# Experts of a two-layer hybrid decoder: gathered rows by block and quarter turned on VectorE, gate-up weights in four parts

## The chip, the cores and the metric

One core of one Trainium2 chip. The metric is the device time of the program in microseconds (us); lower is better. The inputs are float32, and all matmuls run in float32.

## The reference

Two decoder layers over 1024 tokens of width 1024. Layer 0 mixes sliding-window attention with a Mamba-2 scan, layer 1 is a Conformer convolution module. After each mixer comes the part that the change touches, a mixture of 32 SwiGLU experts with hierarchical routing:

```
g_sel = argmax(xt @ w_group + b_group)                    # one of 4 groups per token
eid   = g_sel * 8 + top_k(e_logits of that group, 2)      # two of its 8 experts
gu    = xb @ w_gate_up[e]                                 # 1024 -> 2 x 512
out   = (silu(gu[:, :512]) * gu[:, 512:]) @ w_down[e]     # 512 -> 1024
y[token] += gate * out                                    # 2048 (token, expert) pairs
x = x + y
```

An expert's gate-up weights are 4 MB and its down weights 2 MB; 32 experts in each of two layers make some 400 MB, all of which are read once.

## The kernel before, in words

`moe(k, layer)` runs once per layer, with every engine's program written out in full. Two stages matter here.

**Routing.** TensorE computes the logits (L1416), VectorE the choice of experts, the rank of each pair within its expert and, from a table of tokens by rank that TensorE makes (L1434), two index tables: `hidx`, the row of the normalised tokens `hbuf` (in HBM) that each partition gathers for an expert, and `yidx`, the quarter row of `ybuf` that each partition writes. `row_index` (L1590) makes `hidx` for the fixed experts first and for the others later. `sort_weights` (L1642) then gives `order`, the experts in the order in which they are processed. The first three places (`FIXED`) belong to experts 0, 1 and 2 whatever the router says; the other 29 are sorted by their number of tokens, so that the capacity of each place is known when the program is built: 2, 3 or 4 blocks of 32 tokens (`TB`), 84 blocks in all. Tokens beyond a capacity would go through `over`, a loop that does not run with these inputs. `count_overflow`, `place_overflow` and `index_overflow` (L1656 to L1687) make its tables and set `over_ready`.

**Experts.** For each expert q, 128 whole rows are gathered by GpSimd's queue (`gather`, L1349, three buffers `xg`), turned on TensorE by eight 128x128 transposes (`turn_tokens`, L1450) and brought from PSUM to `xT` by VectorE with the gain `g_exp` (`xT_evacuate`, L1629). Per block n of 32 tokens follow `gate_up(n)` on TensorE (64 matmuls in eight steps of the inner dimension by four groups of columns, with rhs the weights: 32 x 256; L1468), silu on ScalarE (L1294), the product and a 32x32-block transpose on VectorE (`hidden`, L1636 and L1640), `down(n)` on TensorE (L1483), a copy on ScalarE (L1288) and a scatter of quarter rows by GpSimd's queue (L1356). TensorE's order is: all gate-up blocks of expert q, the turning of q + 1, all down blocks of q. A float32 matmul shows twice in the trace, so that one block of gate-up counts 64 and one of down 32.

The weights come through SyncE's queue, in program order: four places for gate-up (`wgu`: `early_gu`, two in `wgu`, and the residual's own room `x_res`, which is parked in HBM meanwhile) and three for down (`wd`). `load_gate_up` (L1182) is one DMA of 4 MB with 32 KB per partition; it waits until the last block of the expert that had the place, four earlier, is through gate-up (`gu_done`). `load_down` (L1185) waits for `d_done` of the expert three earlier. The first load behind the fixed ones needs `order_ready`. The place `wd[2]` holds the router's tables first, so that expert 2's down weights wait for `over_ready`.

```
for q in range(FIXED, BOUND):
    e = sp.value_load(order[0:1, q:q + 1], min_val=0, max_val=NE - 1)
    if q > FIXED:
        sp.wait_ge(gu_done, last_of[gu_user[q]] + 1)
    load_gate_up(sp, e, gu_of[q])
```

## Time and profile before

| what | value |
|---|---|
| median of 3 runs | 2039.64 us (2038.15 to 2040.13) |
| the profiled execution: its span | 2039.7 us |
| TensorE busy | 1861.9 us (91%) |
| VectorE / ScalarE / GpSimd busy | 883.6 / 427.2 / 405.6 us |
| HBM read and written | 504.29 and 43.03 MB |
| experts of layer 0, first gate-up to last down | 546.1 to 1038.1 us |
| experts of layer 1, first gate-up to last down | 1504.0 to 1996.9 us |

The profiled execution has no time of its own beside its span; the span lies 0.1 us from the median, within the spread of the runs, so that the span is taken as the time. The busy share of TensorE is of its matmul queue. In the forty slices of the page each slice is 51 us; the two stretches of experts are the ones in which DMA stands at 9. An idle time that ends with "issue" is one whose end the profile puts down to no other engine.

### The profile page before, as it was taken

What the parts mean: (1) busy time and instruction counts of PE and PEld (TensorE: products, weight loads), DVE (VectorE), ACT (ScalarE), POOL (GpSimd) and SP (SyncE); (2) the same over time, 40 slices, a digit from 0 to 9 for tenths busy, and PEclk for the clock granted to TensorE, in tenths of its full rate; (3) what the DMA queues carried; (4) which work ended last, traced back from release to release, by engine and by line L of the source; (5) the groups of instructions that cost most, each with busy time, mean ns of one, the idle gap of its engine ahead of it and who ended that gap; (6) DMA issues with size and microseconds to landing.
All of it is one profiled execution on the core that took longest, in us unless ns stands there. A gap on an engine that the chain in (4) does not pass through costs nothing. (4 is left out here: it accounts for less than half of the span.)

```text
span 2039.7 us, 46987 instructions
## 1 busy us (share of the span) xinstructions
PE 1861.9 (91%) x20566; PEld 1141.8 (56%) x20566; DVE 883.6 (43%) x1980; ACT 427.2 (21%) x965; POOL 405.6 (20%) x524
## 2 busy tenths in 40 slices
PE   7999999999699999988959999799869999999891
PEld 5677766665466666555645444345546666655551
DVE  3666666564811211111135999893271121121114
ACT  2433332345011111110123122233401111111010
POOL 2211111012122222222122011120112222212120
PEclk9999999999699999999979999899979999999996
DMA  9300000044699999999987446413589999999997
GB/s 324 81 11 1 11 10 10 0 186 168 267 426 426 427 424 427 425 425 427 421 310 195 92 103 134 108 32 134 206 332 422 425 425 426 424 426 428 425 405 276
DMA packets 94256, 541.95 MB, mean 266 GB/s; under 512 B 23366, under 2 KB 46970, under 8 KB 76392
## 3 DMA queue, kind: packets, MB, share of 16 engines
q1 hardware_dynamic: 68376, 479.13, 57.3%
q0 software_dynamic: 23040, 51.43, 9.1%
q10 hardware_dynamic: 2640, 8.44, 1.0%
q8 instruction: 160, 2.62, 0.5%
q14 instruction: 40, 0.33, 0.1%
HBM read 504.29 MB, written 43.03 MB: 268 GB/s over the span
## 5 line engine op out<-in xcount | busy, mean ns | idle before, releaser
L1636 DVE TENSOR_TENSOR acts<-acts,ps 128x128 f32<-128x128 f32 x168 | 66.1, 393 | 781.3 <-ACT acts L1294 780.9
L1356 POOL DMA_INDIRECT y_rows<-rows_in_out,yidx x168 | 166.7, 992 | 747.3 <-ACT rows_in_out L1288 720.5
L1468 PE MATMUL ps<-wgu,xT 128*32 128x256 f32 x5376 | 297.7, 381 | 9.8 <-issue 9.7
L1468 PEld LDWEIGHTS ps<-wgu,xT 128*32 128x32 f32 x5376 | 181.7, 110 | 120.9 <-issue 13.1
L1483 PE MATMUL ps<-wd,acts 128*32 128x256 f32 x3520 | 198.6, 380 | 0.0
L1468 PE MATMUL ps<-x_res,xT 128*32 128x256 f32 x2816 | 159.2, 387 | 16.6 <-issue 16.6
L1294 ACT ACTIVATE acts<-ps 128x128 f32<-128x128 f32 x168 | 46.6, 277 | 608.0 <-PE ps L1468 608.0
L1468 PE MATMUL ps<-early_gu,xT 128*32 128x256 f32 x2560 | 146.7, 389 | 7.9 <-DVE xT L1629 4.1
L1483 PEld LDWEIGHTS ps<-wd,acts 128*32 128x32 f32 x3520 | 110.9, 110 | 74.8 <-issue 6.7
L1468 PEld LDWEIGHTS ps<-x_res,xT 128*32 128x32 f32 x2816 | 96.3, 112 | 77.6 <-issue 22.5
L2232 DVE SCALAR_TENSOR_TENSOR conv<-dd,par,conv 128x256 f32<-128x256 f32 (+1 forms) x255 | 131.4, 589 | 0.2
L1288 ACT ACTIVATE rows_in_out<-ps 128x256 f32<-128x256 f32 x168 | 64.4, 384 | 304.5 <-PE ps L1483 304.5
L1468 PEld LDWEIGHTS ps<-early_gu,xT 128*32 128x32 f32 x2560 | 85.0, 113 | 66.9 <-issue 10.1
L865 PEld LDWEIGHTS ps<-m_hT,early_gu 128*128 128x128 f32 x1024 | 116.1, 192 | 4.7 <-issue 3.3
L865 PE MATMUL ps<-m_hT,early_gu 128*128 128x128 f32 x1024 | 116.9, 275 | 0.7 <-DMA early_gu<-in_w_in 0.7
L1859 PE MATMUL ps<-c_hT,early_wd 128*128 128x512 f32 x256 | 114.4, 600 | 3.4 <-ACT sig L2020 3.2
L1895 PE MATMUL ps<-w_pw,c_hT 128*128 128x512 f32 x256 | 114.4, 602 | 1.5 <-ACT c_hT L2037 1.5
L1867 PE MATMUL ps<-c_hT,early_wd 128*128 128x512 f32 x256 | 112.5, 592 | 0.0
L1483 PE MATMUL ps<-early_wd,acts 128*32 128x256 f32 x1856 | 104.7, 380 | 0.0
L919 PE MATMUL ps<-w_out_sb,m_yT 128*128 128x512 f32 x192 | 86.3, 602 | 0.0
L1859 PEld LDWEIGHTS ps<-c_hT,early_wd 128*128 128x128 f32 x256 | 49.0, 192 | 65.4 <-issue 65.0
L1867 PEld LDWEIGHTS ps<-c_hT,early_wd 128*128 128x128 f32 x256 | 48.7, 190 | 61.2 <-issue 61.2
(354 smaller groups left out, 2225.1 us busy)
## 6 DMA issues: line engine op xcount, KB each, us to landing
wgu<-in_moe_w_gate_up SPq DMA_DIRECT2D x32, 4096.0 KB, 30.8
wd<-in_moe_w_down SPq DMA_DIRECT2D x42, 2048.0 KB, 30.4
early_gu<-in_moe_w_gate_up SPq DMA_DIRECT2D x18, 4096.0 KB, 30.7
x_res<-in_moe_w_gate_up SPq DMA_DIRECT2D x14, 4096.0 KB, 28.8
early_wd<-in_moe_w_down SPq DMA_DIRECT2D x22, 2048.0 KB, 26.4
early_wd<-in_conv_w_pw SPq DMA_DIRECT2D x22, 512.0 KB, 5.5
conv<-prod POOLq DMA_DIRECT2D x20, 512.0 KB, 4.5
x_res<-x_park SPq DMA_DIRECT2D x2, 4096.0 KB, 45.9
```

The source lines that it names most:

```text
L865: mm = pe.matmul(ps[:, bank, (t % 4) * P:(t % 4 + 1) * P], w_x[:, j, t * P:(t + 1) * P], hT[:, j, :], start=(j == 0), stop=(j == KD - 1))
L919: mm = pe.matmul(ps[:, bank, :], attn_T[p][:, j, :] if j < 4 else yT[:, j, :], w_out[:, j, 512 * half:512 * half + 512], start=(j == 0), s ...
L1288: act.activation(y[:, n % YB, :], ps[:, Y + n % 2, 0:D // 4], ACT.Copy).then_inc(y_ready, 1)
L1294: act.activation(sg[:, n % 2, :], ps[:, GU + n % 2, 0:P], ACT.Silu).then_inc(silu_ready, 1)
L1356: pool.indirect_dma_start(out=y_quarters, out_offset=bass.IndirectOffsetOnAxis(ap=yidx[:, tl, q:q + 1], axis=0), in_=y[:, n % YB, :], in_o ...
L1468: mm = pe.matmul(ps[TB * g:TB * g + TB, GU + n % 2, 0:2 * P].rearrange("p (a f) -> p a f", a=2), xT[:, q % 2, j, TB * tl:TB * tl + TB], wg ...
L1483: mm = pe.matmul(ps[TB * g:TB * g + TB, Y + n % 2, 0:D // 4], hhT[:, n % 4, TB * j:TB * j + TB], wd[q % 3][:, j, D // 4 * g:D // 4 * g + D ...
L1636: tt(hh[:, n % 2, :].rearrange("q (k f) -> q k f", k=KF), by_k(sg[:, n % 2, :]), by_k(ps[:, GU + n % 2, P:2 * P]), ALU.mult).then_inc(hh_r ...
L1859: mm = pe.matmul(ps[:, GATE, :], wg[:, p, j, :], hT[:, j, HALF * h:HALF * h + HALF], start=(j == 0), stop=(j == KD - 1))
L1867: mm = pe.matmul(ps[:, LIN + n % 2, :], wa[:, p, j, :], hT[:, j, HALF * h:HALF * h + HALF], start=(j == 0), stop=(j == KD - 1))
L1895: mm = pe.matmul(ps[:, BACK + half, :], yT[:, j, :], w_pw2[:, j, 512 * half:512 * half + 512], start=(j == 0), stop=(j == CT - 1))
L2232: ins = dve.scalar_tensor_tensor(out=out[s], in0=dd[:, s, q + k0:q + k1], scalar=par[:, c, 2 * q - 1 + s:2 * q + s], in1=out[s] if r else ...
```

## The change

- **Blocks instead of experts.** `hbuf` is stored in another order within a row (`stored_row`), so that a quarter of a row holds what 32 partitions need. `gather(n)` now fetches for one block of 32 tokens their four quarter rows, one per group of 32 partitions (128 partitions x 256 values, eight buffers), with `hidx` in the form that `yidx` had. 85 gathers take the place of 32.
- **Turning on VectorE.** `prepare(n)` is a 32x32-block transpose of 128x256 and a product with the gain. It takes the place of TensorE's eight transposes and of `xT_evacuate`. The first five blocks are prepared before the loop (three ahead of `sort_weights`, two behind it), then block n + 5 behind `hidden(n)`.
- **Gate-up in four parts.** Each load is four DMAs of 1 MB (8 KB per partition), each with its semaphore, and each part is loaded as soon as TensorE has used that part of the place's former expert (`gu_part_done`). `gate_up(q)` runs part by part over all blocks of the expert, so that all its blocks are finished in the last part. Four PSUM banks hold them, and four the down blocks.
- **A fourth fixed expert** with room for four blocks; its weights are loaded ahead of `order_ready`. There are 85 blocks in place of 84.
- `index_overflow` runs before the first `hidden`, not behind it.

```diff
-FIXED, FULL, LARGE = 3, 2, 13
-XB, YB = 3, 6
-TURNS, LAST_FULL = 12, 17
+FIXED_CAP = (3 * TB, 3 * TB, 3 * TB, 4 * TB)
+FIXED, FULL, LARGE = len(FIXED_CAP), 2, 12
+PARTS = 4
+XB, YB = 8, 6
+PREPARED = 5
+TURNS, LAST_FULL = 12, 16
...
+        def load_gate_up(sp, e, q):
+            user = gu_user[q]
+            for r in range(PARTS):
+                if user is not None:
+                    if r < PARTS - 1:
+                        sp.wait_ge(gu_part_done, (PARTS - 1) * user + r + 1)
+                    else:
+                        sp.wait_ge(gu_done, last_of[user] + 1)
+                load_gate_up_part(sp, e, gu_of[q], r)
...
             sp.wait_ge(x_parked, 16 * (SQUARED_EARLY + 1))
+            load_gate_up(sp, 3, 3)
             sp.wait_ge(order_ready, 1)
-            down = 2
+            down = FIXED - 1
             for q in range(FIXED, BOUND):
                 e = sp.value_load(order[0:1, q:q + 1], min_val=0, max_val=NE - 1)
-                if q > FIXED:
-                    sp.wait_ge(gu_done, last_of[gu_user[q]] + 1)
-                load_gate_up(sp, e, gu_of[q])
+                load_gate_up(sp, e, q)
                 if q == FIXED:
                     sp.wait_ge(over_ready, 1)
-                else:
-                    sp.wait_ge(d_done, last_of[q - 4] + 1)
+                    load_down(sp, 2, 2)
+                sp.wait_ge(d_done, last_of[q - 4] + 1)
                 load_down(sp, down, (q - 1) % 3)
...
+            def gate_up(q):
+                blocks = range(first_of[q], last_of[q] + 1)
+                if q == 0:
+                    pe.wait_ge(first_gu_loaded, 16)
+                for r in range(PARTS):
+                    if q:
+                        pe.wait_ge(gu_loaded[gu_of[q]][r], 16 * (gu_turn[q] - (gu_of[q] == 0)))
+                    for n in blocks:
+                        if r == 0:
+                            pe.wait_ge(xT_ready, n + 1)
+                            if n >= 4:
+                                pe.wait_ge(hh_ready, n - 3)
+                        for j in range(KD // PARTS * r, KD // PARTS * (r + 1)):
...
+                        if r == PARTS - 1:
+                            mm.then_inc(gu_done, 1)
+                    if r < PARTS - 1:
+                        mm.then_inc(gu_part_done, 1)
...
-            turn_expert(0)
             for q in range(NE):
-                for n in range(first_of[q], last_of[q] + 1):
-                    gate_up(n)
-                if q + 1 < NE:
-                    turn_expert(q + 1)
+                gate_up(q)
                 for n in range(first_of[q], last_of[q] + 1):
                     down(n)
...
+            def prepare(n):
+                dve.wait_ge(gathered[n % XB], 16 * (n // XB + 1))
+                if n >= XB:
+                    dve.wait_ge(gu_done, n - XB + 1)
+                dve.transpose(xT[:, n % XB, :, :].rearrange("p k t -> p (k t)"), xg[:, n % XB, :]).then_inc(xg_turned, 1)
+                dve.wait_ge(xg_turned, n + 1)
+                tt(xT[:, n % XB, :, :], xT[:, n % XB, :, :], g_exp[:, :].unsqueeze(2).to_broadcast([P, KD, TB]), ALU.mult).then_inc(xT_ready, 1)
...
+            for n in range(CAP[0] // TB):
+                prepare(n)
             sort_weights()
-            dve.wait_ge(turned, 1)
-            xT_evacuate(0, CAP[0], xT_ready)
+            for n in range(CAP[0] // TB, PREPARED):
+                prepare(n)
             count_overflow()
             place_overflow()
+            index_overflow()
             for n in range(NB):
                 q, tl = blocks_of[n]
                 hidden(n)
-                if n == last_of[q] and q + 1 < NE:
-                    dve.wait_ge(turned, q + 2)
-                    xT_evacuate((q + 1) % 2, CAP[q + 1], xT_ready)
-                if n == 0:
-                    index_overflow()
+                if n + PREPARED < NB:
+                    prepare(n + PREPARED)
```

How instructions stand on TensorE at the start of the experts of layer 0, in the kernel before (L1437 to L1442 are the index matmuls, L1450 the turning, L1468 gate-up, L1483 down):

```order
L1437 MATMUL ps<-early_gu,wd 128x3
L1440 MATMUL ps<-wd 128x32
L1442 MATMUL ps<-wd,rows_in_out 128x32 x4
L1450 MATMUL ps<-ident,rows_in_out 128x2x4x16 x8
L1468 MATMUL ps<-early_gu,xT 32x256 x96
L1450 MATMUL ps<-ident,rows_in_out 128x2x4x16 x8
L1483 MATMUL ps<-early_wd,acts 32x256 x48
L1468 MATMUL ps<-wgu,xT 32x256 x96
```

and in the change (L1463 and L1467 index, L1484 gate-up, L1502 down):

```order
L1463 MATMUL ps<-early_gu,rows_in_out 128x4 x4
L1467 MATMUL ps<-wd,rows_in_out 128x32 x4
L1484 MATMUL ps<-early_gu,xT 32x256 x96
L1502 MATMUL ps<-early_wd,acts 32x256 x48
L1484 MATMUL ps<-wgu,xT 32x256 x96
L1502 MATMUL ps<-wd,acts 32x256 x48
```

The turning is gone between gate-up and down, and the first index takes four matmuls where it took one. VectorE at the same place, from the second index to the overflow tables, in the kernel before (L1643 and L1644 sort, L1629 the move of expert 0's tokens to `xT`):

```order
L1625 TENSOR_SCALAR yidx<-acts,quarter 128x128
L1643 TENSOR_REDUCE wd<-wd 128x32
L1644 CAST order<-wd 128x32
L1629 TENSOR_TENSOR xT<-ps,g_exp 128x4x96 x2
L1658 MEMSET wd 128x3
```

and in the change (L1643 and L1645 are one `prepare`, L1658 and L1659 the sort):

```order
L1637 TENSOR_SCALAR yidx<-acts,quarter 128x128
L1643 STREAM_TRANSPOSE xT<-rows_in_out 128x256
L1645 TENSOR_TENSOR xT<-xT,g_exp 128x256
L1643 STREAM_TRANSPOSE xT<-rows_in_out 128x256
L1645 TENSOR_TENSOR xT<-xT,g_exp 128x256
L1643 STREAM_TRANSPOSE xT<-rows_in_out 128x256
L1645 TENSOR_TENSOR xT<-xT,g_exp 128x256
L1658 TENSOR_REDUCE wd<-wd 128x32
L1659 CAST order<-wd 128x32
```

The sort stands behind three prepared blocks. SyncE's queue around the first sorted expert, in the change (in the kernel before, the `x_res` load stood behind the TENSOR_LOAD of `order`):

```order
L1230 DMA token_slot<-pad 128x32
L1213 DMA wd<-in_moe_w_down 128x4096
L1200 DMA wgu<-in_moe_w_gate_up 128x2048 x8
L1200 DMA x_res<-in_moe_w_gate_up 128x2048 x4
L1241 TENSOR_LOAD order
```

The load of expert 3's gate-up weights has moved ahead of the wait for the order.

## Rows read from the trace of the kernel before

**Rows 1.** The page of the profile: busy tenths of DMA in forty slices of 51 us
```profile
DMA  9300000044699999999987446413589999999997
```

**Rows 2.** Table of stretches: us, busy (x instructions) per engine, PEclk, DMA share, GB/s
```profile
600.00:700.00 100.00, 100.00 (x1768) 60.62 (x1764) 19.42 (x52) 11.42 (x35) 21.28 (x22) 1.00 1.01 425
...
900.00:1000.00 100.00, 92.88 (x1608) 57.35 (x1604) 16.57 (x44) 10.56 (x32) 21.04 (x21) 0.98 1.01 425
```

**Rows 3.** DMA queues and issues between 610 and 960 us
```profile
q1 hardware_dynamic: 6282, 136.17, 90.9%
...
wgu<-in_moe_w_gate_up SPq DMA_DIRECT2D x12, 4096.0 KB, 37.1
```

**Rows 4.** Timeline of TensorE, layer 0: start us, us, instruction [idle before]
```profile
546.13 12.06 PE L1468 MATMUL ps<-early_gu,xT 128*32 128x256 f32 x192 [1.96 <-DVE xT L1629]
...
863.55 10.57 PE L1468 MATMUL ps<-wgu,xT 128*32 128x256 f32 x192 [1.27 <-issue]
...
897.40 12.22 PE L1468 MATMUL ps<-x_res,xT 128*32 128x256 f32 x192 [5.42 <-issue]
...
1027.53 7.11 PE L1468 MATMUL ps<-early_gu,xT 128*32 128x256 f32 x128 [1.41 <-issue]
1034.43 3.66 PE L1483 MATMUL ps<-wd,acts 128*32 128x256 f32 x64
```

**Rows 5.** Timeline of SyncE's queue, layer 0
```profile
498.25 1.76 SPq L1182 DMA_DIRECT2D wgu<-in_moe_w_gate_up  x2
546.23 0.36 SPq L1182 DMA_DIRECT2D x_res<-in_moe_w_gate_up  x1
...
823.83 0.33 SPq L1182 DMA_DIRECT2D wgu<-in_moe_w_gate_up  x1
```

**Rows 6.** Table of stretches around the start of layer 0's experts
```profile
528.00:530.00 2.00, 0.41 (x1) 0.00 (x0) 1.79 (x4) 0.51 (x1) 0.00 (x0) 0.50 0.01 4
...
556.00:558.00 2.00, 2.00 (x44) 0.96 (x32) 1.65 (x5) 0.00 (x0) 0.00 (x0) 1.00 0.65 270
```

**Rows 7.** Timeline of all engines, layer 0's index and start
```profile
528.52 0.42 DVE L1572 TENSOR_TENSOR wd<-ps,wd 128x256 f32<-128x256 f32 x1 [0.18 <-PE ps L1428]
...
534.87 0.59 PE L1437 MATMUL ps<-early_gu,wd 128*128 128x3 f32 x2 [0.49 <-DVE wd L1587]
...
540.52 1.89 PE L1442 MATMUL ps<-wd,rows_in_out 128*128 128x32 f32 x8
...
544.97 0.18 DVE L1644 CAST order<-wd 128x32 int32<-128x32 f32 x1
...
552.76 0.40 DVE L1636 TENSOR_TENSOR acts<-acts,ps 128x128 f32<-128x128 f32 x1
553.19 0.31 DVE L1640 STREAM_TRANSPOSE acts<-acts 128x128 f32<-128x128 f32 x1
...
556.84 0.17 DVE L1686 CAST pos<-posf 128x16 int32<-128x16 f32 x1
```

**Rows 8.** Chain that ended last, layer 1: start us, us, what
```profile
1556.44 10.36 PE ps L1468 x192
1566.81 1.02 PE ps L1450 x8
1567.83 5.32 PE ps L1483 x96
1573.14 6.91 PE ps L1468 x128
```

**Rows 9.** DMA queues and issues between 1450 and 1462 us
```profile
q10 hardware_dynamic: 144, 1.05, 21.1%
...
h_rows<-prod ACTq DMA_DIRECT2D x1, 1024.0 KB, 3.9
```

**Rows 10.** Table of stretches, end of layer 1's experts
```profile
1995.00:2000.00 5.00, 3.58 (x68) 1.97 (x60) 0.70 (x2) 1.04 (x3) 1.68 (x2) 1.00 0.18 74
```

**Rows 11.** DMA issues between 412 and 430 us
```profile
early_gu<-in_moe_w_gate_up SPq DMA_DIRECT2D x1, 4096.0 KB, 13.2
```

More of the change, by code:

```diff
@@ L72, in capacities @@
     n = NE - FIXED
-    by_place = [3 * TB] * FIXED + [0] * n
+    by_place = list(FIXED_CAP) + [0] * n
     for nth in range(n):
@@ L1225, in _ @@
                 down = sp.value_load(order[0:1, q:q + 1], min_val=0, max_val=NE - 1)
-                sp.wait_ge(gu_done, last_of[gu_user[q]] + 1)
-                load_gate_up(sp, down, gu_of[q])
+                load_gate_up(sp, down, q)
             sp.wait_ge(d_done, last_of[NE - 4] + 1)
@@ L1436, in _ @@
             pe.wait_ge(tab_ready, 1)
-            pe.matmul(ps[:, SPREAD, 0:FIXED], tabT[:], fold[:, 0:FIXED], start=True, stop=True).then_inc(spread, 1)
-            pe.wait_ge(tab_ready, 3)
+            for b in range(P // TB):
+                mm = pe.matmul(ps[:, SPREAD, b * FIXED:(b + 1) * FIXED], tabT_rows[:, b, :], fold[:, 0:FIXED], start=True, stop=True)
+            mm.then_inc(spread, 1)
             pe.wait_ge(fold_ready, 1)
-            pe.matmul(ps[:, TOTALS, 0:NE], tabT[:], fold_sorted[:], start=True, stop=True).then_inc(spread, 1)
             for b in range(P // TB):
@@ L1443, in _ @@
             mm.then_inc(spread, 1)
-            def turn_tokens(buf, done, by_rank=True):
-                for j in range(KD):
-                    columns = ps[:, TRN + j // 4, (j % 4) * P:(j % 4 + 1) * P]
-                    if by_rank:
-                        columns = columns.rearrange("p (b h t) -> p h b t", h=2, t=TB // 2)
-                    mm = pe.transpose(columns, xg[:, buf, j * P:(j + 1) * P], ident[:])
-                mm.then_inc(done, 1)
-            def turn_expert(q):
-                pe.wait_ge(gathered[q % XB], 16 * (q // XB + 1))
-                if q:
-                    pe.wait_ge(xT_ready, 2 * q)
-                turn_tokens(q % XB, turned)
@@ L1496, in over @@
             def over(j):
-                pe.wait_ge(o_gathered, j * 16 + 16)
-                turn_tokens(0, o_turned, by_rank=False)
+                pe.wait_ge(o_ordered, j + 1)
+                for i in range(KD):
+                    mm = pe.transpose(ps[:, TRN + i // 4, (i % 4) * P:(i % 4 + 1) * P], over_by_k[:, i * P:(i + 1) * P], ident[:])
+                mm.then_inc(o_turned, 1)
                 pe.wait_ge(o_xT, j * 2 + 2)
@@ L1657, in count_overflow @@
                 cap = cap_e[:, FIXED:NE]
-                dve.memset(cap_e[:, 0:FIXED], float(CAP[0])).then_inc(dve_link, 1)
-                link.n += 1
+                for e in range(FIXED):
+                    dve.memset(cap_e[:, e:e + 1], float(CAP[e])).then_inc(dve_link, 1)
+                link.n += FIXED
                 link(ts(cap, nth[:], float(FULL + LARGE), float(TB), ALU.is_lt, ALU.mult))
@@ L1709, in over @@
                 tt(over_ih[:], over_slot[:], over_h[:], ALU.add).then_inc(o_index, 1)
+                dve.wait_ge(o_gathered, j * 16 + 16)
+                dve.tensor_copy(over_by_k.rearrange("q (k g l) -> q g k l", k=KD, g=4), stored_row(over_x)).then_inc(o_ordered, 1)
                 dve.wait_ge(o_turned, j + 1)
-                xT_evacuate(0, P, o_xT)
+                for half in range(2):
+                    tt(over_xT[:, 4 * half:4 * half + 4, :], ps[:, TRN + half, :].rearrange("p (k t) -> p k t", k=4),
+                       g_exp[:, 4 * half:4 * half + 4].unsqueeze(2).to_broadcast([P, 4, P]), ALU.mult).then_inc(o_xT, 1)
                 dve.wait_ge(o_silu, j + 1)
```

182 lines of the change are left out of this document (87 added, 95 removed).

## Prediction

> **What bounds the kernel now.** I read the page's forty slices first, since an average over the span hides the stages. DMA stands at 9 in nine slices in a row in the first stretch of experts and in the same way in the second [rows 1]. The table of stretches then puts numbers to it: in layer 0 from 600 to 700 us TensorE is busy all the time, DMA's share is 1.01 at 425 GB/s, and from 900 to 1000 TensorE is busy 92.88 of 100 us while DMA stands at the same 1.01 and 425 GB/s [rows 2]. So two resources run close together, and it is DMA that does not give way. The view of the queues says what it carries: 90.9% weights, a gate-up load of 4096 KB taking 37.1 us from issue to landing [rows 3], far more than its own 4.19 MB / 425 GB/s = 9.9 us, so about two and a half experts' weights stand in the queue all the time.
>
> The timeline of TensorE shows the consequence. Expert 0 starts at 546.13; later TensorE waits ("issue") for 5.42 us before 897.40 and for 1.41 us before its last gate-up at 1027.53 [rows 4]. The load issued at 823.83 [rows 5] is the one used at 863.55, after a wait of 1.27 [rows 4]: asked for 40 us ahead, and still late. So these are waits for weights. An expert of three blocks costs TensorE 10.36 + 1.02 + 5.32 = 16.7 us, the 1.02 being the turning [rows 8]. The change takes the turning away, 31 x 1.02 = 32 us per layer of TensorE's time. If TensorE were the bound, that would be the gain, less one more block (half of 6.91 for gate-up and a third of 5.32 for down, 5.2 us) [rows 8]. But it isn't: the stage ends when the last weights have landed, and a faster TensorE only waits longer. So I count the time of the weight queue, per layer, from the router to the last gate-up load.
>
> **The change, part by part**, in us per layer, plus is slower.
>
> *The queue starts later behind the router: +4.3.* Before, the first sorted load is issued at 546.23 [rows 5], right behind the cast of `order` at 544.97 [rows 7]. Now the first index needs one copy of 512 columns and four matmuls: four such took 1.89 against 0.59 for one, while the copy was made anyway, behind the index [rows 7]. With the waits around them, everything behind moves by 1.5. Three `prepare` stand ahead of the sort. None is in the trace; the transpose of 128x128 took 0.31 and a product of 256 columns 0.42 [rows 7], so with twice the columns I take 0.45 + 0.42 + 0.08 for the semaphore = 0.95, and 2.85 for three (bounds: 0.31 + 0.42 each, and twice the small transpose plus 0.62, so 2.2 to 3.9). The cast comes at 549.3, the issue at 550.5: +4.3. The load also needs TensorE's first quarter of expert 0: start at about 546.3, three blocks' quarter 10.36 / 4 = 2.6, and 1.5 that the half clock costs (12.06 against 10.57 [rows 4]; the clock stood at 0.50 before, [rows 6]), so 550.4, which is as late.
>
> *One gate-up load leaves that queue: -9.9.* Expert 3's weights are asked for at about 515, when DMA still works on the 8.4 MB of gate-up (and 2.1 of down) issued at 498 [rows 5]. DMA then stood at 0.01 from 528 to 530 [rows 6] and the weights idle until 546.23. Its 9.9 us fit into that hole.
>
> *Smaller packets: +7.0.* 28 loads go in rows of 8 KB in place of 32 KB. The nearest row with 8 KB rows is the store of 1.05 MB that took 21.1% of 16 engines in 12 us [rows 9]: 40.5 engine-us, 0.316 per row, 1.26 per 32 KB. The weights in large rows took 90.9% x 16 x 350 = 5090 for 136.17 MB, 1.225 per 32 KB [rows 3]. The difference, 0.04, times 128 rows / 16 engines is 0.3 per load. One is a store and the other a load, so the bounds are 0 and 0.4; I take 0.25, near the row, and 28 of them.
>
> *Gathers: 0.* 85 in place of 32, but of the same filled rows in all, and empty ones are skipped. On GpSimd, whose 22 instructions took 21.28 us [rows 2], 85 + 85 at that price are 165 us of 492. On VectorE 85 x 0.95 = 81 replace some 62 moves of 0.4 to 0.5 in a stage where it is busy 17 of 100 us [rows 2]. Both hide below TensorE; what if not, is a rival.
>
> *Pauses of the queue: +1.7.* Before, DMA fell to 0.65 only at 556 to 558 [rows 6], 0.7 us. Now five `prepare` and all overflow tables stand ahead of the first `hidden`: `over_ready`, at 557.0 before [rows 7], comes at 549.3 + 12.0 - 1.0 (the old move) - 0.75 (the first `hidden`) + 1.9 = 561.5. By then the queue has just finished expert 4's quarters, so that costs nothing. TensorE, through gate-up at 558.2, gets its first down operand at 562.4, 4.2 late, and pays 1.5 for the clock again; expert 3's down weights wait for the end of expert 0's down at 569.2, when the queue has been empty for 2.0. With 0.4 for quarters paced by TensorE: 2.4 - 0.7.
>
> *The engines end more evenly: -2.5.* At layer 1's end DMA falls from full to 0.18 over 1995 to 2000 [rows 10] while the last loads land: the sixteen engines don't have equal work, and a load lands with the slowest. Gathers of whole rows give a row to one engine; quarters give it to four partitions 32 apart. The bounds are 0 and 5, half of what the tail shows; I take the middle.
>
> *The tail: -0.3.* After the last gate-up landed TensorE took 1034.43 + 3.66 - 1027.53 = 10.6 [rows 4]. Now only a quarter of gate-up is left, but the down weights land 2.1 MB / 425 GB/s = 4.9 behind, then 3.66 follow: 8.6, and 1.7 because TensorE has waited and runs at half clock, as after 5.42 of idling (12.22 against 10.57 [rows 4]).
>
> Sum: 4.3 - 9.9 + 7.0 + 1.7 - 2.5 - 0.3 = +0.3 per layer, +0.6 for two. The stores of the rows in another order, an activation cut in two four times in layer 1, and the longer-lived semaphores are hidden by ScalarE's and the conformer's slack and cost nothing (at most 0.3 each if that were gone). On the profiled execution's 2039.7 this gives 2040.3, and since that span stands 0.1 above the median of the runs I give 2040.5, no change. A measurement of this kernel can tell about 0.2%, 4.1 us, from none.
>
> **Two rules of the Trainium skill.** A load of 4096 KB alone on the chip landed 13.2 us after issue [rows 11], and one of 1024 KB in 3.9 [rows 9]; but in the stage loads stand behind one another at 425 GB/s [rows 2], so the fixed part of each hides in the queue, and the sum has 0 for it. "DMA: Bandwidth & Descriptors", section "Bandwidth", asks for DMAs of 1 MiB or more, and its "Anatomy of one DMA" gives 2.0 us plus bytes / 436 GB/s for each. By an estimate from that page four loads of 1 MB, one after another, would take 6 us more than one of 4, 168 us per layer. The parts are at the page's limit, and that is a rival below.
>
> The rows tell that the engines end unevenly, not which has which partition. The same page, "The descriptor swizzle", gives engine = 8 x (partition / 64) + (partition / 4) mod 8. By an estimate from that map and these inputs' token counts the busiest engine's excess falls from 16 to 11 us in layer 0 and from 12 to 9 in layer 1; with that in place of 2.5 the result would be 2037.5. No run so far shows the map.
>
> **The rivals.** *The packets cost nothing and the engines end evenly: faster.* For it speaks that the price of 8 KB rows comes from a store. With 0 and -5 the layer gives 0.3 - 7.0 - 2.5 = -9.2, and half-way, which I hold for more likely, -5: 2030. Chance 0.28.
>
> *The queue pays more: slower.* One mechanism: the weights' queue runs dry early in the stage, while TensorE paces it. Each quarter waits for TensorE, and TensorE for `hidden(0)`, itself behind 18 us of VectorE's own list. If `prepare` is at its bound (3.9 for three, 6.5 for five) and rows of 8 KB at 0.4, then +1.1 + 1.4 + 4.2, and no evening gives 2.5 back: some +9 per layer, up to 2058; I give it 2050. It decides once the first quarter of expert 4 is issued after about 554. Chance 0.22.
>
> *VectorE becomes what each expert waits for: slower.* All blocks of an expert now end within the last part, 0.86 apart, and the first down needs silu, product and transpose, of which the last two took 0.40 and 0.31 [rows 7]: with silu and the waits some 1.3 behind, an estimate. For experts of two blocks this leaves 0.5 of waiting where the turning's 1.02 was; I reckon it hidden, since TensorE needs 85 x 5.2 + 32 x 0.14 + 5.7 + 8 = 460 of 492. The slack is 32 us over 32 experts: it decides once each expert loses 1 us more. At 1.5 more it costs 16 per layer, 2072. Against it: VectorE has 1.7 per block to do where TensorE takes 5.2. Chance 0.08.
>
> *Each part pays its fixed time: slower.* If only 0.3 of the 3.9 - 2.5 = 1.4 showed per part, 28 x 3 x 0.3 = 25 per layer, 2090. Against it stands 425 GB/s with queued loads. Chance 0.05.
>
> **How the numbers follow.** No change has 0.37, and its own range is 2036 to 2045. Faster by over 0.2% is the first rival, 0.28; slower the other three, 0.35. The range leaves out the two dear rivals and the far tail of the first: 2027 to 2057.
>
> **What would show it.** Right: DMA's share 1.0 from about 570 to 1020 in layer 0; the fixed load issued at about 515 and the next at 550.5; TensorE waiting some 30 us per layer, mostly before down; the last gate-up part landing within 3 us of 1028; no turning on TensorE and about 460 us busy. Wrong: TensorE busy to the end (then a stall of the blocks, not DMA, is the bound), a q1 share per byte above 1.26 per 32 KB, DMA gaps beyond 570, or a GB/s away from 425.

## The result: 0.57% slower, and the profile after

| | before | changed |
|---|---|---|
| median, us (lowest to highest, 4 runs each) | 2039.61 (2038.15 to 2040.13) | 2050.78 (2046.99 to 2052.37) |
| profiled execution: span, us | 2039.7 | 2048.6 |
| granted TensorE clock, mean | 0.957 | 0.946 |

The ratio is 1.0057, with a 95% interval of 1.0043 to 1.0071: 11.2 us slower, clear of the 0.2% that a measurement can tell. The forecast was no change (2040.5). The slower side came: inside the whole range of 2027 to 2057, outside the 2036 to 2045 that went with no change, and at the time that I had given to the rival "the queue pays more", though not by its mechanism.

The page's slices of DMA, after. The high digits are as in [rows 1]; the second line, GB/s, is where the two kernels differ, mostly 415 to 418 in the two stretches of experts where 421 to 428 stood, and 405 and 397 early in the first:
```profile
DMA  9200000044899999999987456413599999999997
GB/s 324 80 11 1 11 10 10 0 185 177 320 405 397 416 417 417 418 417 416 422 314 208 87 112 134 108 32 134 201 376 402 416 415 416 417 418 418 417 413 291
```
The table of stretches of the changed kernel (us, busy time of PE, PEld, DVE, ACT and POOL, PE's clock, DMA share, GB/s), against [rows 2], and as its last row the whole of layer 0's experts:
```profile
600.00:700.00 100.00, 99.08 (x1829) 58.97 (x1825) 26.69 (x76) 12.61 (x39) 39.56 (x39) 1.00 1.00 406
900.00:1000.00 100.00, 86.39 (x1456) 54.57 (x1448) 21.00 (x60) 9.94 (x30) 28.37 (x28) 0.91 1.01 418
...
545.00:1045.00 500.00, 463.52 (x8160) 282.52 (x8160) 130.62 (x379) 56.26 (x170) 169.16 (x166) 0.96 0.99 405
```
DMA is as full as before (1.01), but it moves 418 GB/s in place of 425: full and slower. TensorE has less to do (86.39 of 100 us where it had 92.88), and it waits for the rest. The busy share alone would have hidden the loss.

DMA queues and issues of the changed kernel between 610 and 960 us, against [rows 3]:
```profile
q1 hardware_dynamic: 15056, 131.97, 90.9%
...
wgu<-in_moe_w_gate_up SPq DMA_DIRECT2D x40, 1024.0 KB, 33.2
y_rows<-rows_in_out,yidx POOLq DMA_INDIRECT x61, 7.4
```
The weights' queue has the same 90.9% of sixteen engines as before for 131.97 MB in place of 136.17. That is 90.9% x 16 x 350 / (131.97 MB / 32 KB) = 1.264 us per 32 KB, against 1.225.

Start and end of layer 0 on TensorE's timeline of the changed kernel, against [rows 4] (the number in brackets is the idle time before):
```profile
545.15 13.50 PE L1484 MATMUL ps<-early_gu,xT 128*32 128x256 f32 x192 [2.80 <-DVE xT L1645]
560.96 7.07 PE L1502 MATMUL ps<-early_wd,acts 128*32 128x256 f32 x96 [2.31 <-DVE acts L1655]
...
910.73 6.42 PE L1502 MATMUL ps<-wd,acts 128*32 128x256 f32 x64 [5.30 <-issue]
...
1034.37 1.93 PE L1484 MATMUL ps<-early_gu,xT 128*32 128x256 f32 x32 [1.15 <-DMA early_gu<-in_moe_w_gate_up]
1039.29 5.30 PE L1502 MATMUL ps<-wd,acts 128*32 128x256 f32 x64 [2.98 <-issue]
```
TensorE starts a microsecond earlier (545.15, before 546.13) and ends later: its last down is through at 1039.29 + 5.30 = 1044.6, before at 1034.43 + 3.66 = 1038.1. The waits now stand mostly before a down, as 5.30 at 910.73, and the half clock that follows makes a two-block down 6.42 or 5.30 long in place of 3.66.

SyncE's queue at the start, against [rows 5]:
```profile
514.24 2.25 SPq L1200 DMA_DIRECT2D x_res<-in_moe_w_gate_up  x4
550.71 8.50 SPq L1200 DMA_DIRECT2D early_gu<-in_moe_w_gate_up  x4
```
The fixed load went out at 514.24 and the first quarter of expert 4 at 550.71, as forecast (515 and 550.5).

### The profile page after: what moved, and what is told of

Read it like the earlier page. It is cut to its first block and busy times, and to the rows that moved or that the text cites. A ratio compares the mean times of both kernels' runs of the same rounds, so it can differ in the third digit from the quotient of the medians.

```text
span 2048.6 us, 47486 instructions
## 1 busy us (share of the span) xinstructions
PE 1827.3 (89%) x20254; PEld 1122.8 (55%) x20254; DVE 947.5 (46%) x2194; ACT 429.6 (21%) x973; POOL 518.0 (25%) x628
## 5 line engine op out<-in xcount | busy, mean ns | idle before, releaser
L1381 POOL DMA_INDIRECT y_rows<-rows_in_out,yidx x170 | 173.0, 1017 | 614.1 <-ACT rows_in_out L1314 587.3
L1484 PE MATMUL ps<-wgu,xT 128*32 128x256 f32 x5376 | 297.1, 379 | 1.8 <-DMA wgu<-in_moe_w_gate_up 1.8
L1502 PE MATMUL ps<-wd,acts 128*32 128x256 f32 x3520 | 214.3, 401 | 38.1 <-issue 34.0
L1484 PEld LDWEIGHTS ps<-wgu,xT 128*32 128x32 f32 x5376 | 182.8, 110 | 110.0 <-DMA wgu<-in_moe_w_gate_up 4.1
L1484 PE MATMUL ps<-early_gu,xT 128*32 128x256 f32 x3456 | 195.3, 386 | 8.4 <-DVE xT L1645 7.0
L1374 POOL DMA_INDIRECT rows_in_out<-h_rows,hidx x170 | 176.0, 1035 | 75.3 <-issue 51.1
L1502 PEld LDWEIGHTS ps<-wd,acts 128*32 128x32 f32 x3520 | 126.5, 116 | 122.9 <-issue 54.8
L1484 PEld LDWEIGHTS ps<-early_gu,xT 128*32 128x32 f32 x3456 | 120.5, 112 | 79.5 <-issue 11.8
L1502 PE MATMUL ps<-early_wd,acts 128*32 128x256 f32 x1920 | 120.5, 411 | 28.8 <-issue 19.2
L1484 PE MATMUL ps<-x_res,xT 128*32 128x256 f32 x2048 | 113.9, 379 | 2.1 <-DMA x_res<-in_moe_w_gate_up 2.1
L1502 PEld LDWEIGHTS ps<-early_wd,acts 128*32 128x32 f32 x1920 | 69.3, 118 | 78.2 <-issue 33.1
L1484 PEld LDWEIGHTS ps<-x_res,xT 128*32 128x32 f32 x2048 | 68.4, 110 | 45.0 <-DMA x_res<-in_moe_w_gate_up 4.2
## 6 DMA issues: line engine op xcount, KB each, us to landing
wd<-in_moe_w_down SPq DMA_DIRECT2D x42, 2048.0 KB, 28.8
```

Of the source, the lines that this page charges most:

```text
L1374: pool.indirect_dma_start(out=xg[:, n % XB, :], out_offset=None, in_=h_quarters, in_offset=bass.IndirectOffsetOnAxis(ap=hidx[:, tl, q:q + ...
L1381: pool.indirect_dma_start(out=y_quarters, out_offset=bass.IndirectOffsetOnAxis(ap=yidx[:, tl, q:q + 1], axis=0), in_=y[:, n % YB, :], in_o ...
L1484: mm = pe.matmul(ps[TB * g:TB * g + TB, GU + n % 4, 0:2 * P].rearrange("p (a f) -> p a f", a=2), xT[:, n % XB, j, :], wgu[gu_of[q]][:, j, ...
L1502: mm = pe.matmul(ps[TB * g:TB * g + TB, Y + n % YBANKS, 0:D // 4], hhT[:, n % 4, TB * j:TB * j + TB], wd[q % 3][:, j, D // 4 * g:D // 4 * ...
```

## The experiments

All times are medians; the kernel before ran on the same chip beside each, and differences are taken to that one. The packets' times that are quoted are sums over the records in the traces, divided by the sixteen engines. In the diffs `whole` and `quarters` stand for the two ways to issue one gate-up load. The expectations name theories by letters: A, the price is that of short rows; B, that of a load's later start; C, the loss lies elsewhere; D, the price is one per DMA.

**1. Rows of 8 KB alone, in the kernel before.**
```diff
-            sp.dma_start(wgu[p], w_gu[at(e)].rearrange("a p k n -> p (a k) n")).then_inc(gu_loaded[p], 16)
+            for r in range(4):
+                ks = slice(KD // 4 * r, KD // 4 * (r + 1))
+                sp.dma_start(wgu[p][:, ks, :], w_gu[at(e)][:, :, ks, :].rearrange("a p k n -> p (a k) n")).then_inc(gu_loaded[p], 16)
...
```


> The kernel before, with each gate-up load issued as four DMAs of 1 MB with 8 KB rows, all at the time of the one load, on one semaphore; nothing else changed. Theory A: 0.37 us x 29 loads of a layer = +10.7 per layer, 2061, and 417 GB/s in the stage. Theory D, the price is one per DMA and not per row: also slower, about the same. No price for a queued load (as if the changed kernel's slower rate came from its gathers): 2040.

Measured: 2051.01 (before 2039.83), ratio 1.0057, 1.0044 to 1.0070. This one edit costs as much as the whole change, and half of what theory A said. The stretch 1790 to 1930 us, first of the kernel before, then of this one:
```profile
1790.00:1930.00 140.00, 127.49 (x2184) 80.96 (x2180) 22.07 (x61) 14.53 (x44) 31.30 (x31) 0.98 1.01 426
```
```profile
1790.00:1930.00 140.00, 124.88 (x2092) 79.38 (x2084) 22.45 (x60) 13.87 (x42) 29.19 (x29) 0.96 1.01 420
```
426 falls to 420, 1.4% of a stage of some 470 us, 6.6 us per layer; the time shows 11.2 / 2 = 5.6 per layer. The packets of one layer's weights, added up, take 9.1 us more, and the queue stands idle 4.6 us less (the second table of "Where the prediction was right and where it was wrong"), so a part of a slower queue is taken up by what were pauses. Forecast for it in the change were 7.0.

What is dear could still be the row or the DMA, and the durations of single packets tell. Between 610 and 960 us the median packet of 32 KB takes 1213 ns and one of 16 KB (a row of down weights) 611 in the kernel before, one of 8 KB 311 in this run, and the 4-byte packet of which each load has sixteen at its end, one per engine, 9 ns. All lie within 2 ns of 9 ns + 37.6 ns per KB. A load of 4 MB is 8 rows of 32 KB per engine or 32 of 8 KB: 32 x 311 - 8 x 1213 = 248 ns more for the rows, and 3 x 9 = 27 ns for the three further DMAs. So nine tenths of the price are the row's and one tenth the DMA's.

**2. As many DMAs, but long rows**: four strips of 32 partitions in place of four ranges of `k`.
```diff
+            for r in range(4):
+                ps_ = slice(P // 4 * r, P // 4 * (r + 1))
+                sp.dma_start(wgu[p][ps_], w_gu[at(e)][:, ps_].rearrange("a p k n -> p (a k) n")).then_inc(gu_loaded[p], 16)
...
```


> The kernel before, with each gate-up load as four DMAs of 1 MB too, but cut by partitions (32 each), so that rows stay 32 KB. Theory A: as many bytes per row as before, so 2040 +- 4. Theory D (a price per DMA): as slow as with 8 KB rows, 2055 to 2061. If 32 partitions reach only some of the sixteen engines at a time, the queue is uneven within a load but not over four: at most a few us.

Measured: 2974.53 (2934.31 to 3006.25), ratio 1.452 (1.446 to 1.458). None of the theories had this. The stretch 1000 to 1100 us of it:
```profile
1000.00:1100.00 100.00, 58.03 (x848) 33.02 (x844) 8.11 (x22) 6.06 (x18) 14.12 (x14) 0.81 1.01 210
```
DMA is full and moves half: between 610 and 960 us the median packet of 32 KB takes 2514 ns in place of 1213, and those of the down weights, which are loaded whole as before, 1258 in place of 611. So how a load is cut matters far more than the length of its rows, and the time of this run can't separate row from DMA (the packets of experiment 1 do). Why it halves stays open: a strip lies on 32 partitions alone, and it is also one contiguous MB of HBM, which a range of `k` is not.

**3. The changed kernel with whole loads**, except for expert 4's (its first quarter is what starts the sorted queue).
```diff
-            for r in range(PARTS):
-                load_gate_up_part(sp, e, gu_of[q], r)
+            quarters(sp, e, q) if q == 4 else whole(sp, e, q)
```


> The changed kernel, but every gate-up load except the first dynamic one (expert 4) is one DMA with rows of 32 KB. Theory A, the size of the rows: in the changed kernel's stage an 8 KB packet took 316 ns on average, 1265 per 32 KB, where before a 32 KB packet took 1219; 46 ns x 128 rows / 16 engines = 0.37 us per load, 27 loads of a layer on the path, so about 10 us per layer come back: 2050.8 - 20 = 2031, and DMA moves 425 GB/s again. Theory B, the load's later start counts: a whole load waits until its buffer's last user is through gate-up, up to 8 us later than its first quarter did, and the queue gets gaps: 2045 or more, with DMA's share under 1. Theory C, the loss lies elsewhere (start behind the router, conformer): 2050 unchanged.

Measured: 2051.11 (ratio 1.0059, 1.0046 to 1.0072): no gain at all, where A wanted 2031. But the rate did rise. Two stretches of this run:
```profile
1790.00:1930.00 140.00, 120.04 (x2041) 66.23 (x2036) 29.64 (x85) 13.95 (x43) 40.84 (x40) 0.91 1.01 423
...
572.00:580.00 8.00, 7.53 (x141) 4.30 (x137) 4.10 (x15) 1.22 (x4) 0.64 (x1) 1.00 0.61 223
```
and the second of them in the changed kernel:
```profile
572.00:580.00 8.00, 8.00 (x152) 4.64 (x144) 2.68 (x11) 0.83 (x3) 0.65 (x1) 1.00 0.99 412
```
Theory B holds: a whole load waits for the end of its buffer's last user, and at 572 to 580 the queue stands at 0.61 where quarters keep it at 0.99. Quarters buy early issue and pay in rate, about the same amount each. And A was short as well: 423, not 426. A part of the lost rate has nothing to do with the size of rows. By the packets, they take 9.0 us less per layer than in the changed kernel, and the queue stands idle 8.7 us more.

**4. Halves** (rows of 16 KB), the same otherwise.

> The same with two DMAs of 2 MB, rows of 16 KB. Theory A: 16 KB packets took 622 ns before, 1244 per 32 KB against 1219, so 0.2 us of each load's 0.37 stay: about 2050.8 - 2 x 27 x 0.17 = 2042. If only the quarter size is dear: 2031, as with whole loads. Theory C: 2050.

Measured: 2048.39 (1.0044, 1.0032 to 1.0056), and 421 GB/s over 1790 to 1930. In between, in the rate as in the time.

**5. Quarters only while the queue is short** (experts 4 to 8), whole loads behind.
```diff
+            quarters(sp, e, q) if 4 <= q <= 8 else whole(sp, e, q)
```


> The changed kernel, with gate-up in quarters only for the sorted experts 4 to 8, and whole for all others. The kernel with whole loads from expert 5 on moved its weights in 468 to 470 us per layer in place of 478, but its queue stood idle 7 to 11 us more, because a whole load waits for the end of its buffer's last user while little is queued yet. Theory A (rows and gaps are the two prices, and the gaps come only while the queue is short): both gains at once, the weights at about 470.5 and the idle time as in the changed kernel, 7.7 and 1.0: 7 per layer off 2050.8, so 2037. Theory E, whole loads leave gaps at any time: no better than 2050.

Measured: 2044.25 (1.0020, 1.0011 to 1.0029), 4.1 us more than before where the changed kernel had 11.2. The gap at 572 to 580 is gone (410 GB/s) and 1790 to 1930 has 424 GB/s. The sign and half of the size of theory A came. The 7 us that are missing to 2037 are idle time of the queue: the weights' packets took 470.0 and 470.6 us in the two layers, as expected, but the queue stood idle 11.1 and 7.1 us where 7.7 and 1.0 were. More than half of the difference stands 30 to 50 us behind the first row of down weights (10.8 and 6.9 us of idle time, in the changed kernel 9.1 and 2.9): that is the hole behind the router, and loads that are through sooner only lengthen it. Quarters for the last expert too (experiment 11) bring none of them back.

**6. The fixed load late**: issued behind the wait for the order.
```diff
+            sp.wait_ge(order_ready, 1)
             load_gate_up(sp, 3, 3)
-            sp.wait_ge(order_ready, 1)
```


> The changed kernel with the load of its fourth fixed expert issued only behind the wait for the order, where the first sorted load of before stood: two lines exchanged. By my prediction's step the early issue takes one load, 9.9 us, out of the queue per layer: 2050.8 + 20 = 2070. If instead the hole behind the router would be filled by what is late anyway (in the kernel before with 8 KB rows the idle time fell by 4 to 5 us per layer by itself), less: 2060. If the start doesn't set the end, 2051.

Measured: 2062.96 (1.0113, 1.0097 to 1.0128), 12.2 above the changed kernel, so the early load is worth 6.1 per layer (5.8 when each is taken to the kernel before beside it) and not 9.9. The stretch table from 530 us on, of the changed kernel and then of this one:
```profile
530.00:538.00 8.00, 4.00 (x40) 3.03 (x40) 6.51 (x13) 0.00 (x0) 0.00 (x0) 0.50 0.99 412
...
548.00:552.00 4.00, 4.00 (x49) 2.16 (x45) 3.59 (x19) 0.00 (x0) 3.17 (x3) 0.61 0.39 94
552.00:556.00 4.00, 4.00 (x80) 2.56 (x76) 3.69 (x10) 0.00 (x0) 3.30 (x3) 1.00 0.94 361
568.00:572.00 4.00, 4.00 (x84) 2.38 (x76) 0.00 (x0) 0.38 (x1) 3.08 (x4) 1.00 0.95 328
...
620.00:640.00 20.00, 20.00 (x380) 12.02 (x375) 4.20 (x12) 2.37 (x7) 10.26 (x11) 1.00 0.97 373
```
```profile
530.00:538.00 8.00, 4.00 (x40) 3.04 (x40) 6.59 (x10) 0.00 (x0) 0.00 (x0) 0.50 0.01 3
...
548.00:552.00 4.00, 4.00 (x60) 2.30 (x56) 3.69 (x17) 0.00 (x0) 3.09 (x4) 0.74 0.66 203
552.00:556.00 4.00, 4.00 (x80) 2.48 (x76) 3.66 (x11) 0.00 (x0) 3.36 (x3) 1.00 1.00 394
568.00:572.00 4.00, 4.00 (x81) 2.37 (x77) 0.00 (x0) 0.00 (x0) 3.08 (x4) 1.00 1.00 408
...
620.00:640.00 20.00, 20.00 (x376) 12.02 (x372) 4.20 (x12) 2.11 (x7) 10.28 (x11) 1.00 1.02 413
```
The early load fills the hole (412 GB/s against 3 at 530 to 538). But once it has landed nothing stands in the queue but quarters that TensorE paces, and in the three rows from 548 to 572 the changed kernel moves (203 - 94 + 394 - 361 + 408 - 328) x 4 us = 0.9 MB less, in that of 620 to 640 (413 - 373) x 20 us = 0.8 MB: 4.0 us of the queue together, about what is missing to 9.9. So a part of the gain is given back where the queue is short. TensorE is busy all the time in that last row, in both kernels.

**7. Gathers of quarter rows alone, in the kernel before.**
```diff
-                pool.indirect_dma_start(out=xg[:, q % XB, :], out_offset=None, in_=k.hbuf,
+                for g in range(4):
+                    pool.indirect_dma_start(out=xg[:, q % XB, D // 4 * g:D // 4 * (g + 1)], out_offset=None, in_=k.hbuf.rearrange("t (g n) -> (t g) n", g=4),
+                                            in_offset=bass.IndirectOffsetOnAxis(ap=hidx[:, q:q + 1], axis=0), element_offset=D // 4 * g,
...
```


> The kernel before, with each gather of whole rows done as four indirect DMAs of quarter rows (1 KB), with an index times 4 (one operation on VectorE more at each of two places). Loads unchanged. Theory F, gathers in quarter rows slow the weights' packets beside them (32 KB packets took 1231 ns in the changed kernel with whole loads, 1219 before): 1% of 465 us, +4 per layer, 2048, and packets of 1230 ns. Rival G, the 1% comes from something else in the changed kernel (its loads' times, its blocks): packets stay at 1219 and the time at 2040 to 2042.

Measured: 2085.00 (1.0221, 1.0207 to 1.0235), 37 above theory F. As a measurement of the time it failed: 128 gathers per layer, four to a tile, took 27.9 us each to land (22.4 before), and the scatters beside them 28.8 (21.9 before). ScalarE then waited for scatters to land before it could fill their buffers again, a wait that the kernel before does not have. From its waits, 546 to 1090 us (total, times, longest):
```profile
ACT rows_in_out L1288 <- DMA y_rows<-rows_in_out,yidx: 102.8, 16, 12.5
```
TensorE stood behind that, and to a smaller part waited for gathered rows; the queue ran dry with it. Where DMA was full it moved 424 (820 to 960) and 423 (1790 to 1930) against 425 and 426. That speaks for F, but is no proof of it.

**8. Empty gathers**: two indirect DMAs behind each gather of the kernel before, with every index out of bounds.
```diff
+                for c in range(2):
+                    if q:
+                        pool.wait_ge(spared[c], 16 * q)
...
+                                            in_offset=bass.IndirectOffsetOnAxis(ap=pad[:, 0:1], axis=0),
```


> The kernel before with two indirect DMAs more behind each gather (64 per layer), all of whose indices are out of bounds, so that they move nothing: about as many more instructions of GpSimd as the change adds (53). Theory F1, it is the number of indirect DMAs (their descriptors, written and read) that slows the weights' packets: 423 GB/s, 32 KB packets at 1230 ns, +3 per layer, 2046. Theory F2, it is the 1 KB rows that they fetch: 425.5 GB/s, 1219 ns, 2040.

Measured: 2113.46 (1.0358, 1.0344 to 1.0372); the time failed again as a test, and for an instructive reason. GpSimd's groups from 610 to 960 us, with the idle time before them:
```profile
L1357 POOL DMA_INDIRECT spare<-h_rows,pad x40 | 40.1, 1002 | 169.0 <-DMA spare<-h_rows,pad 165.9 <-issue 3.0
```
and the DMA issues of the same stretch:
```profile
spare<-h_rows,pad POOLq DMA_INDIRECT x40, 17.3
```
An indirect DMA that moves nothing takes 17.3 us to land, and the wait for the one before it held up GpSimd. The rate answers the question, though. The stretch 1790 to 1930 us:
```profile
1790.00:1930.00 140.00, 130.72 (x2252) 77.43 (x2248) 23.18 (x64) 14.37 (x45) 44.50 (x44) 0.96 1.01 423
```
423 GB/s with 32 KB rows, as in experiment 3 and not 426. So it is the further indirect DMAs that take 0.6% off the weights' rate, not the 1 KB rows (theory F1); in proportion to their number it is not, as the 96 more of experiment 7 took no more. Of some 470 us that is 2.8 per layer.

**9. Whole-row gathers and TensorE's turning, with the rest of experiment 5**: fixed expert, gate-up by parts in PSUM banks 2 to 5, quarters for experts 4 to 8.

> A mixture: the kernel before with its gathers of whole rows and its turning on TensorE, and of the change only the fourth fixed expert, gate-up by parts over all blocks of an expert (PSUM banks 2 to 5), and quarter loads for experts 4 to 8, whole ones for the rest. Theory F (gathers in quarter rows cost 0.6% of the rate: 423 GB/s with whole loads in the changed kernel, 425.5 before): 425 GB/s returns, 2.8 us per layer off the 2044.2 of the same loads in the changed kernel, and about as much where the first expert starts earlier (one index matmul, no turning on VectorE ahead of the order): 2034 to 2038, below both kernels. Rival G (the rate falls because of the order in which TensorE reads or of the fixed load): 423 GB/s again, 2042. Rival H, TensorE's turning, 32 us per layer, is what then bounds: TensorE busy throughout and 2045 or more.

Measured: 2043.75 (1.0020, 1.0011 to 1.0030). The stretch 1790 to 1930 us:
```profile
1790.00:1930.00 140.00, 135.63 (x2360) 84.22 (x2356) 23.89 (x65) 15.96 (x48) 33.77 (x34) 0.99 1.01 426
```
426 GB/s: the rate is back with 32 gathers in place of 85, by parts and with the fixed load, so G falls. But TensorE is busy 135.63 of 140 us here and entirely from 600 to 900, and at 600 to 700 DMA's share is 0.98 with 399 GB/s: the queue's early loads now wait for TensorE. By the packets, set to equal bytes, this kernel has 1.7 us less of them per layer than that of experiment 5 and 1.3 more of idle time. H takes most of what F gives. Without the change's turning on VectorE, TensorE is too slow for this queue early in the stage.

**10. One piece at the end of the layer, in the kernel before**: the last expert's gate-up in quarters, worked by parts.

> The kernel before with one piece of the change alone, at one place: the last expert's gate-up is loaded in four quarters and worked by parts over its two blocks; everything else as before. Before, TensorE stood 1.4 us (layer 0) and 2.5 us (layer 1) for the last load and then needed its whole gate-up and down, 10.6 and 12.1 us behind that load's landing. If the end of a layer is set there: only a quarter (1.9) is left when the last part lands, the down weights land some 5 us behind the gate-up weights, then 3.66 or 5.3 for down: 8.6 to 10.2 in place of 10.6 and 12.1, so 0.4 to 3.5 off each layer, 2035 to 2039. If the tail isn't on the path, or the clock takes all of it: 2040.

Measured: 2040.02 against 2038.72 (1.0005, 0.9996 to 1.0014): no change. On TensorE it did what was meant. Its timeline, layer 0:
```profile
1032.28 3.66 PE L1508 MATMUL ps<-wd,acts 128*32 128x256 f32 x64 [1.59 <-DVE acts L1667]
1047.76 0.73 PE L1947 MATMUL ps<-ident,c_rows 74*128 74x74 f32 x4 [11.81 <-PEq L120]
```
The experts end at 1035.9, 2.2 before 1038.1 [rows 4]; the next stage begins at 1047.76, where the kernel before has 1048.17. In layer 1 TensorE is 3.9 earlier, but the last stores of `y_rows` take 8.2 us to land in place of 5.3. So the layer ends with its last DMAs and not with TensorE's last down; why these land later isn't shown.

**11 and 12. Quarters at both ends**, in the kernels of experiments 5 and 9.

> The changed kernel with quarter loads at both ends of the stage only (experts 4 to 8 and 31), whole ones between (with 4 to 8 alone: 2044.2). In layer 1 of that kernel TensorE waited 4.35 us for the last whole load and then took 10.01 for its gate-up. With quarters the end comes 2 to 4 us earlier in layer 1 and 1 to 2 in layer 0: 2039 to 2041, level with before. The remaining price is that of the indirect DMAs, 2.5 GB/s of 425. If quarters at the end bring nothing: 2044.

> The mixture with whole-row gathers and turning on TensorE (2043.75), with quarter loads for the last expert too. Its tails are as in the one above (3.5 and 3.2 us of waiting, 8.80 for the last gate-up), so 1.5 to 3 per layer: 2038 to 2041. If TensorE's early part (busy 100% up to 900 us) had set the end instead, 2043.

Measured: 2042.86 (1.0022, 1.0013 to 1.0031) and 2044.76 (1.0034, 1.0022 to 1.0046). Over the kernel before beside them that is 4.1 and 6.0 us, where experiments 5 and 9 had 4.1 and 4.2: neither is better than without. Both miss what I expected; that it is for the reason of experiment 10 fits, but isn't shown. No version found here beats the kernel before; the best of the changed design is 0.2% behind it.

## Where the prediction was right and where it was wrong

The time fell within the range, but not by the working: the range was wide for the sake of the rivals, and the sum itself missed. The forecast's sum was +0.3 per layer, the result is 11.2 / 2 = +5.6. Two of the experiments stand between the two kernels and split it, per layer:

| | edit between the two | measured | forecast |
|---|---|---|---|
| before to experiment 1 | 8 KB rows | +5.6 | +7.0 |
| experiment 1 to 6 | router, `prepare`, gathers, parts, more even engines, tail | +6.0 | +4.3 + 1.7 + 0 - 2.5 - 0.3 = +3.2 |
| experiment 6 to the change | fixed load early | -6.1 | -9.9 |

The error of 5.3 is, as nearly as this tells, 2.8 for the second line, 3.8 for the fixed load and -1.4 for the rows. With each kernel taken to the one before beside it, the second and third lines are +5.8 and -5.8; the intervals leave about 2 us open in either.

The packets show what lies behind the times. From the first row of down weights of a layer's stage to the last, in us for layer 0 / layer 1 (198.0 to 198.7 MB of large packets each, which leaves about 1 us open):

| kernel | packets of weights / 16 engines | idle time of DMA |
|---|---|---|
| before | 464.8 / 465.0 | 15.1 / 9.3 |
| experiment 1, 8 KB rows | 474.2 / 474.0 | 11.2 / 4.1 |
| experiment 6, fixed load late | 477.5 / 477.4 | 14.2 / 8.7 |
| the change | 478.8 / 478.1 | 7.4 / 0.9 |
| experiment 3, whole loads | 468.5 / 470.4 | 14.2 / 11.5 |
| experiment 5, first quarters | 470.0 / 470.6 | 11.1 / 7.1 |
| experiment 9, own turning | 467.2 / 468.5 | 11.0 / 9.7 |

Per layer the change adds 13.5 us of packets and takes away 8.0 of idle time, together +5.5; the time showed +5.6. The forecast had +7.0 of packets and 4.3 + 1.7 - 9.9 = -3.9 of idle time.

**Smaller packets: right.** 7.0 forecast, 5.6 in the time, 6.6 in the rate and 9.1 by the packets, of which pauses that shrank took up 4.6. The price read off the store in [rows 9] was good: 0.316 us for 8 KB, and loads took 0.311. A load came to 0.29 where I took 0.25, and 31 are split, not 28. The first rival, that packets cost nothing, falls.

**Gathers: 0. This step failed.** I counted their bytes and GpSimd's time and found both hidden, and they are. What I left out is what each indirect DMA does to the queue beside it: with 53 more per layer 426 GB/s become 423, shown by experiment 8's empty ones and, the other way round, by experiment 9. In us per layer this is 2.8 worked out from the rate, and 1.7 by the packets of experiments 5 and 9, set to equal bytes; the time alone was never measured.

**More even engines: -2.5. Not seen, and not settled.** The end of layer 1's weights, of the kernel before:
```profile
1986.00:1990.00 4.00, 3.52 (x39) 2.00 (x42) 0.00 (x0) 0.00 (x0) 0.00 (x0) 0.57 0.68 288
1990.00:1994.00 4.00, 4.00 (x80) 2.54 (x76) 0.70 (x2) 0.28 (x1) 0.00 (x0) 1.00 0.35 147
```
and of the changed kernel, whose last weights land some 12 us later:
```profile
1998.00:2002.00 4.00, 2.14 (x40) 1.23 (x32) 1.39 (x4) 0.56 (x2) 0.00 (x0) 1.00 0.62 257
2002.00:2006.00 4.00, 2.73 (x52) 2.06 (x56) 0.00 (x0) 0.38 (x1) 0.08 (x1) 1.00 0.25 105
```
DMA falls off in the same way, 0.68 and 0.35 against 0.62 and 0.25. No evening of the engines can be seen there, and the estimate by the Trainium skill's map of descriptors ("DMA: Bandwidth & Descriptors", section "The descriptor swizzle") of 5 and 3 us less excess isn't borne out. No experiment isolated it. With 2.8 for the gathers in the second line of the first table, 3.2 are left for start, pauses, evening and tail together; forecast were 3.2 with the evening and 5.7 without it. The second table speaks for the start: from experiment 1 to 6 the idle time rose by 3.8 per layer, where 4.3 + 1.7 = 6.0 had been put down for start and pauses.

**One load leaves the queue: -9.9. The mechanism was right, but this term was mis-sized by 3.8, the largest error of the sum.** The hole was filled as I said, but in the forecast the load's whole length counted as gain. It is 6.1 (experiment 6): the idle time falls by 7.3 per layer and the packets take 1.0 more, since the queue behind is then short and goes at TensorE's pace.

**The start: the times were right.** The first quarter went at 550.71 (forecast 550.5), the cast of `order` came at 547.80 (549.3), the first down at 560.96 (562.4). The cast was 1.5 earlier than forecast and the load was not, so that it went when TensorE was through its first quarter, the second of the two conditions that I had named. What they cost wasn't measured apart.

**The tail: right in size, but little of it reaches the end.** From the last gate-up part to the end TensorE took 1044.6 - 1034.4 = 10.2 (10.6 before, forecast 0.3 less). In experiment 10 TensorE ended 2.2 and 3.9 us earlier at this place, and 0.4 of the 2.2 reached the next stage; the time did not fall.

**The rivals.** "The queue pays more" gave the time to within 1 us and was wrong in its mechanism: its point of decision, a first quarter later than 554, wasn't reached, and rows of 8 KB were not at their bound. VectorE's price per expert didn't come: 0.31 us of waiting before a down and TensorE 463.52 us busy, as forecast. A fixed time per part didn't come: experiment 1 has 93 more DMAs per layer and costs 5.6, of which the DMAs' own part is 93 x 9 ns = 0.8. The rule of the Trainium skill that a DMA should have 1 MiB or more ("DMA: Bandwidth & Descriptors", section "Bandwidth") and its fixed 2.0 us for each ("Anatomy of one DMA"), which by the estimate from that page meant 168 us per layer for parts in turn, don't bear on loads that queue: 5.6 were measured. The Trainium skill gives those 2.0 us for DMAs that GpSimd issues, and these loads are SyncE's; and the 3.9 us for 1024 KB that I set beside them are a store's [rows 9]. The list of what would prove me wrong did its work: a price above 1.26 per 32 KB (1.264), a rate away from 425 (418) and gaps beyond 570 (0.97 at 620 to 640) were all on it. Of the signs of being right, the issues, TensorE's 463.52 us and its waits before a down came; the last gate-up part, used at 1034.37 after a wait for it, landed 6 us behind 1028 and not within 3.

## What to carry to other kernels

- Where DMA is the bound, read its GB/s beside its share. Both kernels stand at 1.01; the loss of 1.6% (418 for 425) is in the rate alone. Then add up the packets' time and the idle time apart: a slower queue hides a part of its price in pauses that shrink. Count what shares the queue too: more indirect DMAs cost the loads beside them something, even when they move nothing (426 to 423 GB/s).
- Splitting a load buys an earlier issue and pays in rate. The first is worth something only while the queue is short, the second is paid on every load; so if a load is split at all, then there and nowhere else (2050.8 against 2044.3). A gain at one end of a queue is worth less than its length when what stands behind it then waits for the other engine (6.1 for 9.9).
- Work taken from an engine that is close to the bound but not at it is worth nothing by itself; here 32 us of TensorE's time per layer bought none, though without it the other parts of the change would have run into TensorE.

## What the runs showed of the hardware

- In a full stage a packet takes 9 ns + 37.6 ns per KB on its engine: 311 ns for 8 KB, 611 for 16 KB, 1213 for 32 KB, 9 for 4 bytes (medians, 610 to 960 us, kernel before and experiment 1). Four rows of 8 KB take 31 ns more than one of 32 KB.
- Loads in strips of 32 partitions halve DMA's rate at a full share: 210 GB/s against 425 (experiment 2), with the same bytes, the same number of DMAs as experiment 1, and longer rows.
- A gather in a full stage lands after 22.4 us where the gate-up loads beside it have 32 KB rows. With rows of 8 KB and nothing else changed it takes 10.1 (experiment 1, 610 to 960 us):
```profile
rows_in_out<-h_rows,hidx POOLq DMA_INDIRECT x23, 10.1
```
  In the changed kernel it takes 7.7, and an empty one beside 32 KB rows 17.3. Of short rows this is the one benefit seen, and nothing here needed it.
- SyncE's own issue slows down in the changed kernel as the stage goes on. From the timeline of its queue:
```profile
778.68 0.33 SPq L1213 DMA_DIRECT2D wd<-in_moe_w_down  x1
...
806.28 2.61 SPq L1213 DMA_DIRECT2D wd<-in_moe_w_down  x1
...
868.46 9.27 SPq L1213 DMA_DIRECT2D wd<-in_moe_w_down  x1
```
  One issue of down weights takes 2 us and more in place of 0.33. With whole loads it stays at 0.33 or 0.34 (600 to 1010 us of the kernel before and of experiments 3 and 5), in experiment 1 it rises to 9.48, so it comes with the shorter loads, of which more stand in the queue; no run isolates it further. It cost nothing that shows, since DMA's share was 1.01 then.
